# Two transformer blocks with product-key experts: 32 of the 256 tokens take their chosen expert rows by gather, the other 224 stay dense, and the dense values are computed with the table as the stationary operand

## The reference, cut to what matters

```python
def peer_ffn(h, w_query, sub_keys, expert_u, expert_v):      # 8 heads, 16384 experts, 16 chosen per head
    q = jnp.einsum('bsd,dk->bsk', h, w_query).reshape(B, S, 8, 2, 128)
    sc = jnp.einsum('bshpc,hpnc->bshpn', q, sub_keys)
    s1, i1 = lax.top_k(sc[..., 0, :], 16)
    s2, i2 = lax.top_k(sc[..., 1, :], 16)
    # the 256 sums s1+s2, their 16 best: idx = i1*128 + i2, gates = softmax
    u = expert_u[ec]                                         # (tokens, 8, 16, 1024)
    a = jax.nn.gelu(jnp.einsum('cd,chkd->chk', xc, u), approximate=False) * wc
    return jnp.einsum('chk,chkd->cd', a, expert_v[ec])
...
x = x + gt2[:, None, :] * peer_ffn(h2, ...)                  # then rmsnorm with final_g
```

## Time and profile before

| what | value |
|---|---|
| median of 3 runs | 2153.9 us (2152.68 to 2154.63) |
| span of the profiled execution | 2151.7 us |
| PE busy | 2102.5 us, 98% of the span |
| DVE busy | 1598.0 us, 74% |
| ACT busy | 1296.9 us, 60% |
| POOL busy | 100.4 us, 5% |
| moved by DMA | 408.41 MB, mean 190 GB/s |

### The profile page before, as it was taken

The page is one execution under the profiler, slowest core; times in us unless marked ns, Lnnn a source line. Parts: engine busy times, 40 slices in busy tenths (PEclk is TensorE's granted clock), DMA queues, the critical chain, the costliest instruction groups (busy, mean ns, idle before and its releaser), DMA issues.

```text
span 2151.7 us, 35772 instructions
## 1 busy us (share of the span) xinstructions
PE 2102.5 (98%) x13364; PEld 1882.0 (87%) x13364; DVE 1598.0 (74%) x3454; ACT 1296.9 (60%) x2430; POOL 100.4 (5%) x136
## 2 busy tenths in 40 slices
PE   7999999999999999999989998999999999999998
PEld 5998988889999888888789998888899998888886
DVE  3777679898889767777757555798988887555556
ACT  3455556567999655555556544565679995554454
POOL 0000001203000000000000000021120000000000
PEclk9999999999999999999989999999999999999999
DMA  9755566665444567888644524666654445565663
GB/s 359 265 203 165 188 191 191 191 191 170 130 130 123 183 240 274 290 288 290 224 148 139 202 90 146 189 188 194 187 169 125 129 129 177 189 193 193 195 194 129
DMA packets 106172, 408.41 MB, mean 190 GB/s; under 512 B 11537, under 2 KB 11921, under 8 KB 101137
## 3 DMA queue, kind: packets, MB, share of 16 engines
q1 hardware_dynamic: 99168, 362.86, 52.8%
q10 hardware_dynamic: 6832, 43.27, 5.7%
HBM read 405.04 MB, written 1.05 MB: 189 GB/s over the span
## 4 chain that ended last, share of the span: by engine, by line
PE 89%; DVE 6%; ACT 3%; issue 1%; POOL 1%; DMA 0%; ACTq 0%; DVEq 0%
PE PB L494 20%; PE PB L495 19%; PE PB L496 19%; PE PB L872 11%; PE PB L870 6%; PE PB L846 6%; PE PB L803 2%; PE PB L869 2%; DVE WL L1618 1%; ACT WH L1161 1%; PE PB L802 1%; PE PB L821 1%; ACT AR L1320 1%; DVE AR L1643 1%; PE PB L560 1%
## 5 line engine op out<-in xcount | busy, mean ns | idle before, releaser
L1618 DVE TENSOR_TENSOR WL<-RING,WH 128x1024 fp32r<-128x1024 f32 x651 | 801.8, 1232 | 413.7 <-ACT WH L1161 410.8
L1161 ACT ACTIVATE WH<-RING 128x1024 fp32r<-128x1024 f32 x651 | 686.7, 1055 | 430.7 <-PE PB L496 415.7
L494 PE MATMUL PB<-WH,HX 128*128 128x512 f32 (+2 forms) x1344 | 492.3, 366 | 6.9 <-DVE HX L1697 3.2
L495 PE MATMUL PB<-WL,HX 128*128 128x512 f32 (+2 forms) x1344 | 489.6, 364 | 0.0
L496 PE MATMUL PB<-WH,HX 128*128 128x512 f32 (+2 forms) x1344 | 489.6, 364 | 0.0
L494 PE MATMUL PB<-HX,WH 128*128 128x256 f32 x1440 | 426.0, 296 | 8.1 <-DVE HX L1697 5.7
L495 PE MATMUL PB<-HX,WH 128*128 128x256 f32 x1440 | 410.5, 285 | 0.0
L496 PE MATMUL PB<-HX,WL 128*128 128x256 f32 x1440 | 410.1, 285 | 0.0
L872 PE MATMUL PB<-HX,WH 128*128 128x512 f32 x1092 | 389.0, 396 | 0.0
L870 PE MATMUL PB<-HX,WL 128*128 128x256 f32 x1248 | 322.4, 279 | 0.0
L494 PEld LDWEIGHTS PB<-WH,HX 128*128 128x128 f32 x1344 | 254.7, 190 | 51.3 <-DVE HX L1697 3.7
(11 more groups left out here) (238 smaller groups left out, 2008.1 us busy)
## 6 DMA issues: line engine op xcount, KB each, us to landing
RING<-in_u SPq DMA_DIRECT2D x256, 512.0 KB, 3.7
RING<-in_v SPq DMA_DIRECT2D x256, 512.0 KB, 4.3
RING<-in_win SPq DMA_DIRECT2D x90, 512.0 KB, 4.0
AR<-in_wr ACTq DMA_DIRECT2D x36, 1024.0 KB, 7.3
RING<-in_wq SPq DMA_DIRECT2D x32, 512.0 KB, 3.7
AR<-in_wm SPq DMA_DIRECT2D x8, 1024.0 KB, 16.1
RING<-in_wout SPq DMA_DIRECT2D x16, 512.0 KB, 3.7
AR<-in_wm ACTq DMA_DIRECT2D x4, 1024.0 KB, 7.7
```

The lines of the kernel that those rows point to most:

```text
L494: e.matmul(o, ah, bh, start=start, stop=False)
L495: e.matmul(o, ah, bl, start=False, stop=False)
L1161: e.activation(hi(t), raw(("w", t), words(t)), ACT.Copy).then_inc(s_hi, 1)
L1618: e.tensor_tensor(lo(t), raw(("w", t), words(t)), hi(t).bitcast(F32), ALU.subtract).then_inc(s_lo, 1)
```

## The change

- `SP = 32`: the last 32 tokens leave the dense stages; `T = 224` columns remain. The wide form uses 448 and 224 columns (`dense`, `both_parts`), the narrow form 224, and 56 gate groups remain (`NQ = T // 4`). `JG` is 84: 83 wide tiles, 45 narrow ones.
- Those 32 tokens: their h rows are turned by 8 transposes behind the first query columns and copied to HROW, POOL copies them to all four groups of 32 partitions. When the choice is done, DVE packs index and gate (PK), POOL spreads them by 4 small transfers (SPX), then issues 64 gathers per block (`indirect_dma_start`), each of 128 rows of 4 KB: 32 from u, 32 from v, in 3 buffers (GB). For every gather DVE has one instruction of 128 x 1024: a product with row sum for u, a multiply-accumulate into ACC for v. `SPARSE` places them in the v stage, one in 1.86 tiles. ACT applies gelu to the 128 x 32 sums in the middle. A matmul with SEL at the end adds the four partition groups.
- The v stage has the table stationary and the tokens moving: `weighted`, 8 pieces of 128 output columns, each with one matmul of 448 and one of 224 columns, into all eight banks. The sums lie with output columns on partitions, so ACT and DVE scale them with the gate as a per-partition scalar (YT) and PE transposes them back (`back`) before they are added to X. `bcast` in the v stage goes.
- Half of the second block's modulation row sums (12 chunks) move from the first block's v stage to the projections of the second block (`late_sums`), their loads to POOL's queue. Places in SBUF and of two small loads are changed to fit.

```diff
-JG = 79
-NQ = S // 4
+JG = 84
+SP = 32
+T = S - SP
+GK = SP * NK // 128
+N_GATHER = 2 * GK
+N_BUF = 3
+NQ = T // 4
...
+SPARSE = {}
+for _m in range(N_GATHER):
+    SPARSE.setdefault(2 + _m * 119 // N_GATHER, []).append(_m)
...
-IN_V = {V_FIRST + 4 * (i + (i > 0)): 24 + i for i in range(24)}
+N_IN_V = 12
+IN_V = {V_FIRST + 8 * i + 4 * (i > 0): 24 + i for i in range(N_IN_V)}
...
+                        if c == 0:
+                            for k in range(KT):
+                                r = e.transpose(PB[4 + k // 4][0:SP, 128 * (k % 4):128 * (k % 4) + 128], HT[:, k, T:S],
+                                                ident)
...
                                     if m == 0:
-                                        e.matmul(PB[b][:, :], wh[:, m, :], HX[:, m, :], start=True, stop=False)
-                                    r = e.matmul(PB[b][:, 0:256], wl[:, m, :], HH[:, m, :], start=False, stop=False)
+                                        e.matmul(both_parts(b), wh[:, m, :], dense(m), start=True, stop=False)
+                                    r = e.matmul(PB[b][:, 0:T], wl[:, m, :], HH[:, m, 0:T], start=False, stop=False)
...
-                    for a in range(2):
-                        tok = slice(128 * a, 128 * a + 128)
-                        for h in range(2):
-                            cs = slice(512 * h, 512 * h + 512)
-                            r = three(PB[4 + 2 * a + h][:, :], HH[:, k, tok], HL[:, k, tok], wh[:, cs], wl[:, cs],
-                                      n == 0, False)
+                def weighted(c, n, start, stop):
+                    k, cs = n % 4, slice(128 * c, 128 * c + 128)
+                    e.matmul(both_parts(c), hi(n_v + n)[:, cs], dense(k), start=start, stop=False)
+                    return e.matmul(PB[c][:, 0:T], lo(n_v + n)[:, cs], HH[:, k, 0:T], start=False, stop=stop)
...
+                for c in range(KT):
+                    for n in range(NK - 1 if c < 2 else NK - NW, NK):
+                        r = weighted(c, n, False, n == NK - 1)
...
+                    gathered(c).then_inc(s_fp, 1)
+                    if c == KT - 2:
+                        back(0)
+                back(1)
...
+                def gathered(m):
+                    M = N_GATHER * blk + m
+                    buf, k = GB[:, M % N_BUF, :], m % GK
+                    e.wait_ge(s_gb[M % N_BUF], 16 * (M // N_BUF + 1))
...
+                    if m < GK:
+                        r = e.tensor_tensor_reduce(buf, buf, HROW, 1.0, 0.0, ALU.mult, ALU.add, DOT[:, k:k + 1])
...
+                    r = e.scalar_tensor_tensor(out=ACC, in0=buf, scalar=GEL[:, k:k + 1], in1=ACC, op0=ALU.mult, op1=ALU.add)
...
-                    if n == 11:
-                        bcast(1 + 2 * blk, gate)
+                    for m in SPARSE.get(n, ()):
+                        gathered(m)
...
+                for c in range(KT):
+                    e.wait_ge(s_fp, 8 * blk + c + 1)
+                    e.wait_ge(s_yp, 8 * blk + c + 1)
+                    e.scalar_tensor_tensor(out=YT[:, c, 0:T], in0=PB[c][:, 0:T], scalar=gate[:, c:c + 1],
+                                           in1=YT[:, c, 0:T], op0=ALU.mult, op1=ALU.add).then_inc(s_yt, 1)
...
+                for m in range(N_GATHER):
+                    M = N_GATHER * blk + m
+                    if M >= N_BUF:
+                        e.wait_ge(s_spent, M - N_BUF + 1)
+                    e.indirect_dma_start(
+                        out=GB[:, M % N_BUF, :], out_offset=None, in_=ur if m < GK else v,
...
+            for g in range(24 + N_IN_V, 48):
+                e.wait_ge(s_mdv, max(N_IN_V, g - 25))
+                e.dma_start(row_chunk(g), row_source(g)).then_inc(chunk_landed(g)[0], 16)
```

More of the change, by code:

```diff
@@ L281, in two_block_kernel @@
         s_pair = sem("s_pair")
+        s_hr, s_hc, s_hd, s_pk, s_sx, s_sel = sem("s_hr"), sem("s_hc"), sem("s_hd"), sem("s_pk"), sem("s_sx"), sem("s_sel")
+        s_gb = [sem(f"s_gb{i}") for i in range(N_BUF)]
+        s_spent, s_gel, s_yp, s_yt, s_xt = (
+            sem("s_spent"), sem("s_gel"), sem("s_yp"), sem("s_yt"), sem("s_xt"))
         s_ah, s_al, s_fp, s_tx, s_tg, s_fin = sem("s_ah"), sem("s_al"), sem("s_fp"), sem("s_tx"), sem("s_tg"), sem("s_fin")
@@ L909, in peer @@
-                    r.then_inc(s_used, 1)
-                    if n == 14:
-                        bcast(1 + 2 * blk, (1, 2))
-                def last(a, h, ms):
-                    tok, cs = slice(128 * a, 128 * a + 128), slice(512 * h, 512 * h + 512)
-                    for n in ms:
-                        k = n % 4
-                        r = three(PB[4 + 2 * a + h][:, :], HH[:, k, tok], HL[:, k, tok],
-                                  hi(n_v + n)[:, cs], lo(n_v + n)[:, cs], False, n == NK - 1)
-                    return r
+                    for c in (0, 4, 5, 6, 7, 1, 2, 3):
+                        if n == 0 and c == 1:
+                            e.wait_ge(s_act, NK * (blk + 1))
+                            e.wait_ge(s_tm, times_done(blk, NK - 1))
+                        r = weighted(c, n, n == 0, False)
@@ new lines, in peer, with gathered, back @@
+                    r.then_inc(s_used, 1)
+                def gathered(c):
+                    return e.matmul(PB[c][:, 2 * T:2 * T + SP], ACC[:, 128 * c:128 * c + 128], SEL[:, :], start=True,
+                                    stop=True)
+                def back(h):
+                    for a in range(2):
+                        for q in range(4):
+                            e.wait_ge(s_yt, 8 * blk + 4 * h + q + 1)
+                            r = e.transpose(PB[2 * h + a][:, 128 * q:128 * q + 128],
+                                            YT[:, 4 * h + q, 128 * a:128 * a + 128], ident)
+                        r.then_inc(s_xt, 1)
@@ L921, in peer @@
                 e.wait_ge(s_al, NK * blk + NK - 1)
                 tile_ready(e, n_v + NK - 2)
-                last(0, 0, range(NK - NW, NK - 1))
-                last(0, 1, range(NK - NW, NK - 1))
+                for c in range(2):
+                    for n in range(NK - NW, NK - 1):
+                        weighted(c, n, False, False)
                 e.wait_ge(s_al, NK * blk + NK)
                 tile_ready(e, n_v + NK - 1)
-                last(0, 0, [NK - 1]).then_inc(s_fp, 1)
-                last(0, 1, [NK - 1]).then_inc(s_fp, 1)
@@ L1388, in peer @@
                         fill(n_q + 2 * c + 1)
+                    if c == 0:
+                        for h in range(2):
+                            e.wait_ge(s_hr, 2 * blk + h + 1)
+                            copy(HROW[0:SP, 512 * h:512 * h + 512], PB[4 + h][0:SP, :], s_hc)
                     if c == 1:
@@ L1485, in peer @@
                 fill(n_v + NK - NW)
-                for a in range(2):
-                    for h in range(2):
-                        i = 4 * blk + 2 * a + h
+                for c in range(KT):
+                    e.wait_ge(s_fp, 8 * blk + c + 1)
+                    e.wait_ge(s_mod, 9 if blk else 7)
+                    e.activation(YT[:, c, :], PB[c][:, T:T + S], ACT.Copy, scale=gate[:, c:c + 1]).then_inc(s_yp, 1)
+                for h in range(2):
+                    for a in range(2):
+                        i = 4 * blk + 2 * h + a
                         cs = slice(512 * h, 512 * h + 512)
@@ L1744, in vector_program @@
                 fill(n)
+            e.wait_ge(s_kc, 16)
+            e.tensor_reduce(SEL[:, :], ident.rearrange("p (g t) -> p t g", t=SP), AX, ALU.add).then_inc(s_sel, 1)
             e.wait_ge(s_used, W_F - 1)
@@ L2077, in peer @@
                             pass
+                        ts = slice(128 - SP, 128)
+                        own.done(own.n)
+                        i1, i2, gt = (GI[ts, s, 1, :].rearrange("p (g k) -> p g k", k=GK) for s in (1, 2, 0))
+                        e.wait_ge(s_gi, 2 * blk + 2)
+                        e.tensor_copy(PK[ts, :, 1, :], gt)
+                        e.scalar_tensor_tensor(out=PK[ts, :, 0, :].bitcast(U32), in0=i1, scalar=128.0, in1=i2, op0=ALU.mult,
+                                               op1=ALU.add).then_inc(s_pk, 1)
                         chosen(blk)
@@ L2154, in vector_program, with late_sums @@
             fill(W2_Q)
-            bcast(2, MC[:, 64:72])
+            late_next = [24 + N_IN_V]
+            def late_sums():
+                for j in range(2):
+                    row_sum(late_next[0], j)
+                late_next[0] += 1
+            bcast(1, MC[:, 64:72])
             for c in range(2):
@@ L2209, in vector_program @@
             log_rest(2)
+            late_sums()
             fill(W2_VS + 2)
```

220 lines of the change are left out of this document (136 added, 84 removed).

## The result

| | before | after |
|---|---|---|
| median | 2154.27 us (2152.68 to 2154.95, 4 runs) | 2071.57 us (2068.94 to 2074.18, 4 runs) |
| ratio | | 0.9616, 95% interval 0.9602 to 0.9629 |
| span of the profiled execution | 2151.7 us | 2069.8 us |

A forecast was written before the change was run, and what follows sets the result against it. PE's pace through its columns was taken as the bound: 2151.7 less 73.8 (u) and 58.4 (v), plus 16.4 (ends and late chunks), gives 2035.9; with 2.2 for the median, 2038 us. Range 2015 to 2092.

The forecast's parts named there:

- A: Rival, chance 0.21: DVE falls behind, 13 us more per block in wide u, 15 in first v; 2079 with both.
- B: Rival, chance 0.12: transfers set the pace in the first block's v stage, at 343 GB/s; 2062 us in all.
- 0.1114 as the floor: PE's matmuls: 224 columns cost 0.1114 us, the distance seen at 16 columns, instead of 0.1067 by column count.
- C: Rival, chance 0.05: 224 columns are no cheaper than 256 at 0.120 us; 24 us per block, 2086 in all.
- D: Rival, chance 0.05: no floor, 0.1067 us for 224 columns, and stalls fully covered; 2005 to 2020 in all.
- At 412 it costs nothing: First v stage: asks 377 GB/s; the start's 412 GB/s was taken as available, so no time was charged for transfers.
- The 4 us charged for stalls behind DVE's work: First block's v stage: 4 us added for runs of DVE peaks that PE's lead does not cover.
- 2 us a block were charged: Wide u stage: 2 us of stalls added to 213.1, since DVE's load of about 210 us nearly equals PE's; 215 us.
- a gate group: Narrow u stage: 56 gate groups at 0.975 us each beside 45 tiles, 174.9 us, and 177 with stalls.
- Ends: Behind each v stage: 5.7 us more per block, 1 for transposes, and 3 for late chunks; 16.4 us together.
- Rival E: Rival, chance 0.07: v stage paced by serial POOL gathers, slower than before from 6.2 us each; 2249 at 7 us.
- the forecast's signs: In the v stage: DVE idle before low parts, ended by ACT's rounding, would show the main forecast, chance 0.50.

The follow-up runs named there:

- short_gather_sums: Changed kernel with DVE's 64 instructions per block on gathered rows cut from 1024 to 16 elements, all gathers kept: 2069.32 us.
- late_held: Changed kernel with ten chunks loaded in halves, gathers respaced, and late chunks held until the first v stage's end: 2071.06 us.
- wide_u_full_columns: Changed kernel with the wide u products back at 512 and 256 columns: 2106.07 us.
- no_gather_transfers: Changed kernel with 61 of 64 gathers per block left out, DVE's instructions still running on the buffers: 2063.33 us.
- thin_chunks: Changed kernel with the first v stage's 12 modulation chunks loaded on 8 of 128 partitions, row sums kept: 2061.95 us.
- dense_256: Changed kernel with all 256 tokens dense and no gathers, keeping the turned v product, new ending and late chunks: 2189.86 us, 1.0174 of before.

## Why the prediction was right, and where its sum was not

The total fell into the range because the prices of A and B had been put into it; the places that they name both cost time, at other sizes. Little was luck of signs: of nine stretches only the tail and the start came out shorter than forecast.

**PE's rates: right.** 0.1114 as the floor, 2.518 a wide tile, 2.49 forecast for 2.51. The last is about 2 us per v stage too low. The distance of 16 columns and that of 224 are the same 0.1114, which bears out a floor; that the weight load makes it was taken for granted and not shown. Rivals C (0.120) and D (0.1067) are refuted by the starts.

**The gathers' transfers: the step that failed.** "At 412 it costs nothing; ... so I take the upper row and nothing." It cost 8 to 12 us: the first v stage has 336.9 for 324.6, and 8.2 to 9.6 us of the whole go when gathers or chunks go. Rival B named the place and the wait (ACT idle ended by table loads), with 24 us as its price. The row of 412 GB/s was 30 us long; over 280 us the after kernel got 354, short_gather_sums 358. The lower end, 343, came from dividing a rate by its share, and that is not sound either: the shares 0.78, 0.94 and 0.95 went with 261, 354 and 358 GB/s, that is 335, 377 and 377 a full share. The Trainium skill, "DMA: Bandwidth & Descriptors", section "Where 436 GB/s comes from", puts the HBM side of one core at about 358 GB/s, half of a stack's 716 for two cores, and the estimate from it was 12 us. The size agrees with the 12.3 measured, but the runs don't show a ceiling at that figure: between 776 and 828 us of this very stage the after kernel got 377 GB/s, about what it asks for, and late_held stalls at 346. What lies under it is shown as far as landing times: many loads of tiles come about as late as four slots allow or later, ACT and with it DVE's low parts wait for them, and the stalls are there only where gathers and chunks are both in flight. Which queue gives way to which there stays open; three rearrangements that thinned or smoothed the demand moved the stalls and did not remove them. The 4 us charged for stalls behind DVE's work may be in part real (short_gather_sums); they were not told apart.

**Wide u: the stall term was mis-sized.** 2 us a block were charged, 7.4 measured (wide_u_full_columns). I read DVE's load over the whole stage (about 210 of 215) and not tile by tile: two choosing steps with the tile's own work take 2.89 us, over PE's 2.52, at ten tiles of a block. This is rival A in part. Its size (13 us a block) was too large. In the second v stage it did not come at all: PE is at work through every tile. In the first, PE's idle time was ended by low parts, A's sign, but DVE's own idle time before these was ended by ACT's rounding (34.5 us) and ACT's by table loads (71.8 us).

**Narrow u: a gate group was mis-sized.** 180.7 us less 45 x 24 x 0.1114 leaves 60.4 for 56 groups, 1.08 each for 0.975. Between 529.34 and 530.48 lies 1.14, of which 0.11 is the matmul, so this group, with no wait in the profile, costs 1.03; the rest is waits for DVE's one-hots (2.8 us in the first block) and edges.

**Ends: right in the middle, too dear at the tail.** Between the blocks 298.7 for 298.3, the 12 late chunks with it. The tail's 5.6 too much and the 2.7 us that the second v stage shows in its last tiles are one thing: part of the new ending runs between the last table products, and I had put all of it behind them.

**Rival E: out.** 128 gathers, one wait of 1.2 us. A gather lands in 8.2 us (median), POOL has the next two under way, and 4.6 us each was asked for. The Trainium skill, "SBUF — State Buffer", section "Who interferes with whom", ties GpSimd's transfers to VectorE's two-port modes. By that rule nothing should lengthen them here. The waits agree, but the issue on POOL was lengthened: 115 of the 128 started while DVE was at a low part and took 1.98 us (median), the 13 others 0.93. The same section also has a VectorE instruction with two SBUF inputs contend with a GpSimd instruction that reads SBUF, and a low part has two; that rule fits the trace better, though no run here changes the low part to test it. So E's reason, that the two contend, was right, and its price wrong.

**The signals named ahead** did their work: "wrong if the v stage keeps over 335 us" was met by the first block (338.2), and the trace showed the sign written for B, ACT idle ended by table loads. It showed A's and the forecast's signs in the same stage too, since the waits form one chain; no_gather_transfers and thin_chunks decided, not the signs.

## What to carry to other kernels

Take a transfer rate for a stage from a stretch as long as the stage, and compare landing times with how far ahead the slots let you ask; a median that fits can hide a quarter of loads that do not. When the engine that sets the pace gets faster by a tenth, go through the second engine's work tile by tile: an average of 95% means that its peaks and each of its waits now show, and moving them about, twice, won nothing. And ask of each half of a change what it brings alone: here one half costs 36 us, and the other brings 118 on top of it.

## What the runs showed of the hardware that was not expected

- The same two lines of code, without a wait in either stage, ran at 2.83 us a tile in the first v stage of dense_256 and 2.77 in the second, evenly over all tiles (0.3535 and 0.3467 a pair of 512 and 256 columns). The granted clock reads 1.00 in both; DMA moved 227 and 183 GB/s. It is not explained; it is 7 us.
- In that pair's short form (448 and 224) the short matmul holds the next start for about 0.10 us, under the 0.1114 of 224 columns alone, and the long one 0.21, over the 0.200 of the columns' rule. The sum is 0.3131. A floor per matmul holds for a row of equal ones, and for a mixed pair only the sum should be trusted.
- A gather of 128 rows of 4 KB keeps POOL for 1.98 us (median, up to 3.41) at its issue, but for 0.93 where no DVE instruction of 1024 elements is running at its start. In short_gather_sums 101 of 128 issues start so, and its median is 0.94. In all 115 cases the DVE instruction is the low part, which reads two tensors (RING and WH). In the second block its landing fell from 8.2 to about 6.4 us when DVE's sums were cut to 16 elements, with the same traffic (317 GB/s for 320); in the first block, at 358 GB/s, it didn't (8.2 for 8.4). The 1.04 us less at the issue can be part of these 1.8, but the issue was as short in the first block; no run here separates it from the earlier release of the buffers.
